# The scan's inverse products as 32x32 blocks, with GpSimd placing only the diagonal blocks of zt

## What is computed

```python
lower = jnp.where(strict, jnp.einsum('bnhid,bnhjd->bnhij', k_beta, k) * decay, 0.0)
t_inv = lax.linalg.triangular_solve(lower + eye, eye, left_side=True, lower=True, unit_diagonal=True)
...
def step(s, inp):
    q_i, val_i, kc_i, at_i, gl_i, kt_i = inp
    v_new = val_i - jnp.einsum('bhcd,bhde->bhce', kc_i, s)
    o = jnp.einsum('bhcd,bhde->bhce', q_i, s) + jnp.einsum('bhij,bhje->bhie', at_i, v_new)
    s = s * jnp.exp(gl_i)[..., None, None] + jnp.einsum('bhcd,bhce->bhde', kt_i, v_new)
    return s, o
xs = tuple(jnp.moveaxis(a, 1, 0) for a in (q_dec, value, k_cum, attn, g_last, k_tail))
_, o = lax.scan(step, s0, xs)
```

## Time and profile before

| | us |
|---|---|
| median of 3 runs (2006.83 to 2012.97) | 2008.74 |
| the profiled execution | 2008.84 |
| its span | 2007.1 |
| PE busy | 1934.2 (96%) |
| DVE busy | 1034.9 (52%) |
| ACT busy | 588.4 (29%) |
| POOL busy | 545.0 (27%) |

### The profile page before, as it was taken

The page is one execution under the profiler, slowest core; times in us unless marked ns, Lnnn a source line. Parts: engine busy times, 40 slices in busy tenths (PEclk is TensorE's granted clock), DMA queues, the critical chain, the costliest instruction groups (busy, mean ns, idle before and its releaser), DMA issues.

```text
span 2007.1 us, 29418 instructions
## 1 busy us (share of the span) xinstructions
PE 1934.2 (96%) x11744; PEld 1562.7 (78%) x11744; DVE 1034.9 (52%) x1363; ACT 588.4 (29%) x952; POOL 545.0 (27%) x336
## 2 busy tenths in 40 slices
PE   8999999999999999999889999999999999999994
PEld 6777787677788887888667687788888888888883
DVE  2747643864459601777676429324242424242437
ACT  3434533334221211656421311222111212122112
POOL 1221122211122313344143824321212222121203
PEclk9999999999999998999999999999999999999997
DMA  6345672336553582686553632121212121211102
GB/s 161 62 101 129 165 171 81 84 93 167 137 145 100 133 235 85 188 239 202 180 172 116 205 105 61 35 63 31 63 31 63 31 63 32 62 38 56 48 5 84
DMA packets 339847, 211.86 MB, mean 106 GB/s; under 512 B 166140, under 2 KB 310140, under 8 KB 337696
## 3 DMA queue, kind: packets, MB, share of 16 engines
q1 hardware_dynamic: 264176, 156.38, 28.1%
q10 hardware_dynamic: 75568, 54.04, 9.4%
HBM read 151.27 MB, written 59.06 MB: 105 GB/s over the span
## 4 chain that ended last, share of the span: by engine, by line
PE 45%; DVE 3%; POOL 1%; DMA 1%; ACT 0%; issue 0%; SPq 0%; DVEq 0%; ACTq 0%
PE b_ps L154 11%; PE b_ps L155 11%; PE b_ps L156 11%; PE f_ps L154 4%; PE f_ps L155 4%; PE f_ps L156 4%; DMA o_raw<-in_w_out 1%; DVE l_stats L2277 1%; POOL x1lo L1764 1%; DVE y L2289 0%; DVE y L2274 0%; PE f_ps L1845 0%; POOL wo_lo L1770 0%; PE f_ps L1807 0%; POOL x1lo L1756 0%; PE f_ps L1882 0%
## 5 line engine op out<-in xcount | busy, mean ns | idle before, releaser
L154 PE MATMUL bank<-xhi,w_hi 128*128 128x512 f32 x976 | 393.2, 403 | 2.3 <-POOL w_lo L433 1.5
L155 PE MATMUL bank<-xlo,w_hi 128*128 128x512 f32 x976 | 385.8, 395 | 0.0
L156 PE MATMUL bank<-xhi,w_lo 128*128 128x512 f32 x976 | 385.7, 395 | 0.0
L433 POOL TENSOR_TENSOR w_lo<-w_raw,w_hi 128x1024 fp32r<-128x1024 f32 x61 | 167.9, 2753 | 600.3 <-ACT w_hi L799 600.3
L2249 DVE TENSOR_TENSOR bw_raw<-bw_raw,b_ps 128x512 f32<-128x512 f32 x42 | 28.9, 688 | 388.4 <-PE b_ps L156 380.1
L154 PEld LDWEIGHTS bank<-xhi,w_hi 128*128 128x128 f32 x976 | 183.7, 188 | 48.4 <-POOL w_lo L433 3.4
L156 PEld LDWEIGHTS bank<-xhi,w_lo 128*128 128x128 f32 x976 | 183.4, 188 | 44.5
L155 PEld LDWEIGHTS bank<-xlo,w_hi 128*128 128x128 f32 x976 | 183.6, 188 | 43.8 <-issue 1.7
L2257 DVE TENSOR_TENSOR y<-y,f_ps 128x512 f32<-128x512 f32 x320 | 200.5, 684 | 0.5
L1792 POOL TENSOR_TENSOR bw_split<-ff_raw_down,ff_hi_down 128x1024 fp32r<-128x1024 f32 x22 | 53.3, 2422 | 526.7 <-ACT ff_hi_down L2050 526.7
L154 PE MATMUL f_ps<-ff_hi_down,ff_hhi 128*128 128x512 f32 x352 | 142.3, 404 | 3.6 <-DVE ff_hlo L2268 3.6
(11 more groups left out here) (324 smaller groups left out, 3443.7 us busy)
## 6 DMA issues: line engine op xcount, KB each, us to landing
w_raw<-in_w_in ACTq DMA_DIRECT2D x61, 512.0 KB, 4.4
op<-opnd SPq DMA_DIRECT2D x16, 1152.0 KB, 5.5
u<-work ACTq DMA_DIRECT2D x68, 256.0 KB, 4.0
b_gate<-u SPq DMA_DIRECT2D x24, 512.0 KB, 3.6
ff_raw_gate<-in_ffn_gate SPq DMA_DIRECT2D x22, 512.0 KB, 4.0
ff_raw_up<-in_ffn_up SPq DMA_DIRECT2D x22, 512.0 KB, 5.4
ff_raw_down<-in_ffn_down SPq DMA_DIRECT2D x22, 512.0 KB, 5.9
opnd<-work SPq DMA_DIRECT2D x20, 512.0 KB, 5.7
```

The lines of the kernel that those rows point to most:

```text
L154: pe.matmul(out, w_hi, x_hi, start=first, stop=False)
L155: pe.matmul(out, w_hi, x_lo, start=False, stop=False)
L156: return pe.matmul(out, w_lo, x_hi, start=False, stop=last)
L433: pool.tensor_tensor(w_lo[b][:, :, :], w_raw[b][:, :, :], as_f32(w_hi[b][:, :, :]), ALU.subtract).then_inc(w_lo_done, 1)
```

## The change

The products are made with the 32x32 blocks themselves. The first one takes `corner` and `packed` as they were loaded, on partitions 0 to 31 and 64 to 95 (`upper`), and writes partitions 32 to 63 and 96 to 127 (`lower`); the second goes the other way. `join`, `inv` and `place_inverse` are gone. `ps_y` and `ps_z` have columns of their own in the bank. ACT copies the two 32-partition pieces of `ps_y`, DVE copies the two pieces of `ps_z` into the corner of `zt` instead of adding, and POOL copies the diagonal blocks into `zt`, whose zeros are set once at the start of the scan, where chunk 0 is now placed too. The second product waits for the `zt` copies of the chunk before; the transpose did so until now. Writers of `zt` wait for `ps_w` of two chunks back. Core of the diff:

```diff
-def place_inverse(pool, c, tiles, join_done, inv_done):
-    op, ar, sv, wv, packed, corner, inv, join = tiles
-    b, d = c % 2, c % DEEP
-    for k in (0, 64):
-        pool.tensor_copy(join[b][k:k + 32, :, NB:2 * NB], corner[d][k:k + 32, :, :]).then_inc(join_done, 1)
-    pool.wait_ge(join_done, c * 2 + 2)
-    for q in range(4):
-        rows, t0 = slice(32 * q, 32 * q + 32), NB * (q % 2)
-        pool.tensor_copy(inv[b][rows, :, :, t0:t0 + NB], packed[d][rows, :, :, :]).then_inc(inv_done, 1)
...
-            for b in range(2):
-                pool.memset(inv[b][:, :, :, :], 0.0).then_inc(early_cleared, 1)
-                pool.memset(join[b][:, :, :], 0.0).then_inc(early_cleared, 1)
...
-            place_inverse(pool, 0, early, early_join, early_placed)
...
-        ps_y = ps_z = ps_yz[:, 0:NPAIR * C].rearrange("p (u s) -> p u s", u=NPAIR)
+        ps_y, ps_z = (ps_yz[:, n * NPAIR * NB:(n + 1) * NPAIR * NB].rearrange("p (u s) -> p u s", u=NPAIR) for n in range(2))
+        upper = [slice(64 * e, 64 * e + NB) for e in range(2)]
+        lower = [slice(64 * e + NB, 64 * e + 2 * NB) for e in range(2)]
...
-                if c:
-                    pe.wait_ge(zt_done, c)
...
-                pe.wait_ge(join_done, c * 2 + 2)
-                pe.wait_ge(inv_done, c * 4 + 4)
+                pe.wait_ge(inv_landed[d], c // DEEP * 48 + 48)
                 for u in range(NPAIR):
                     for e in range(2):
-                        h = rwkv_rows(e)
-                        last = pe.matmul(ps_y[h, u, :], join[b][h, u, :], inv[b][h, 0, u, :], start=True, stop=True)
+                        last = pe.matmul(ps_y[lower[e], u, :], corner[d][upper[e], u, :], packed[d][upper[e], 0, u, :], start=True, stop=True)
...
-                pe.wait_ge(y_done, c + 1)
+                pe.wait_ge(y_done, c * 2 + 2)
                 pe.wait_ge(vt_done, c + 1)
+                if c:
+                    pe.wait_ge(zt_done, c * 2)
                 for u in range(NPAIR):
                     for e in range(2):
-                        h = rwkv_rows(e)
-                        last = pe.matmul(ps_z[h, u, :], y[b][h, u, :], inv[b][h, 1, u, :], start=True, stop=True)
+                        last = pe.matmul(ps_z[upper[e], u, :], y[b][lower[e], u, :], packed[d][lower[e], 1, u, :], start=True, stop=True)
...
-                dve.wait_ge(inv_done, c * 4 + 4)
-                dve.tensor_tensor(zt[b][:, :, :], ps_z, inv[b][:, 1, :, :], ALU.add).then_inc(zt_done, 1)
+                if c == 0:
+                    dve.wait_ge(zt_cleared, 2)
+                if c >= 2:
+                    dve.wait_ge(mm_w, c - 1)
+                for e in range(2):
+                    dve.tensor_copy(zt[b][upper[e], :, NB:2 * NB], ps_z[upper[e], :, :]).then_inc(zt_done, 1)
...
-                act.activation(y[b][:, :, :], ps_y, ACT.Copy).then_inc(y_done, 1)
+                for e in range(2):
+                    act.activation(y[b][lower[e], :, :], ps_y[lower[e], :, :], ACT.Copy).then_inc(y_done, 1)
...
+            for b in range(2):
+                pool.memset(zt[b][:, :, :], 0.0).then_inc(zt_cleared, 1)
+            pool.wait_ge(zt_cleared, 2)
...
-                if c:
-                    place_inverse(pool, c, tiles, join_done, inv_done)
+                if c >= 2:
+                    pool.wait_ge(mm_w, c - 1)
+                for e in range(2):
+                    for k, half in enumerate((upper[e], lower[e])):
+                        pool.tensor_copy(zt[b][half, :, k * NB:(k + 1) * NB], packed[d][half, 1, :, :]).then_inc(inv_done, 1)
```

More of the change, by code:

```diff
@@ L260, in scan_tiles @@
     packed, corner = loads("inv_packed", [2, NPAIR, NB]), loads("inv_corner", [NPAIR, NB])
-    inv, join = ([sb(f"{name}{b}", [P] + shape) for b in range(2)] for name, shape in (("inv", [2, NPAIR, C]), ("join", [NPAIR, C])))
-    return op, ar, sv, wv, packed, corner, inv, join
+    return op, ar, sv, wv, packed, corner
 def load_chunk(sp, c, tiles, opnd, xinv, landed, inv_landed):
-    op, ar, sv, wv, packed, corner, inv, join = tiles
+    op, ar, sv, wv, packed, corner = tiles
     b, row = c % DEEP, opnd[c]
@@ L387, in project_and_prepare @@
         inv_landed, inv_cleared, inv_stored = sem("inv_landed"), sem("inv_cleared"), sem("inv_stored")
-        early_landed, early_inv, early_cleared, early_join, early_placed = (sem("early_" + n) for n in ("landed", "inv", "cleared", "join", "placed"))
+        early_landed, early_inv = (sem("early_" + n) for n in ("landed", "inv"))
         inv_step = [sem(f"inv_step{k}") for k in range(2)]
@@ L434, in _ @@
             local.sweep(pool)
-            *_, inv, join = early
-            pool.wait_ge(inv_stored, 16 * 4 * R)
-            for b in range(2):
-                pool.memset(inv[b][:, :, :, :], 0.0).then_inc(early_cleared, 1)
-                pool.memset(join[b][:, :, :], 0.0).then_inc(early_cleared, 1)
-            pool.wait_ge(early_cleared, 4)
-            pool.wait_ge(early_inv, 48)
-            place_inverse(pool, 0, early, early_join, early_placed)
-            pool.wait_ge(early_placed, 4)
         @block.sync
@@ L1148, in scan_and_attend @@
         local.enter_context(nc.sbuf_tensor("scan_tiles", [P, sum(math.prod(t.shape[1:]) for group in tiles for t in group)], F32))
-        op, ar, sv, wv, packed, corner, inv, join = tiles
+        op, ar, sv, wv, packed, corner = tiles
         causal, attn = two("causal", [8, C]), two("attn", [2, 2, C])
         tok_g = two("tok_g", [2, 2, GD])
-        y, zt = two("y", [NPAIR, C]), two("zt", [NPAIR, C])
+        y, zt = two("y", [NPAIR, NB]), two("zt", [NPAIR, C])
         r_rw, r_g, w_g = two("r_rw", [4, C]), two("r_g", [2, GD]), two("w_g", [2 * GD])
@@ L1170, in scan_and_attend @@
         mm_m, mm_a, mm_y, mm_z, mm_r, mm_w, mm_s, mm_o = (sem("mm_" + n) for n in "mayzrwso")
-        masked, attn_done, inv_done, join_done, tok_done, y_done, zt_done = (
-            sem(n) for n in ("m_masked", "attn_done", "inv_done", "join_done", "tok_done", "y_done", "zt_done"))
+        masked, attn_done, inv_done, tok_done, y_done, zt_done = (
+            sem(n) for n in ("m_masked", "attn_done", "inv_done", "tok_done", "y_done", "zt_done"))
+        zt_cleared = sem("zt_cleared")
         r_rw_done, r_g_done, w_done, s_sum_done, s_rw_done, dec_done, s_g_done, o_done = (
@@ L1221, in _ @@
                     sp.wait_ge(mm_o, c - DEEP + 1)
-                    sp.wait_ge(zt_done, c - DEEP + 1)
+                    sp.wait_ge(zt_done, 2 * (c - DEEP + 1))
+                    sp.wait_ge(inv_done, 4 * (c - DEEP + 1))
                     load_chunk(sp, c, tiles, opnd, xinv, landed[b], inv_landed[b])
@@ L1288, in state @@
                 yield
-                pe.wait_ge(zt_done, c + 1)
+                pe.wait_ge(zt_done, c * 2 + 2)
+                pe.wait_ge(inv_done, c * 4 + 4)
                 pe.wait_ge(r_rw_done, c + 1)
@@ L1521, in _ @@
         def _(pool):
-            pool.sem_inc(join_done, 2)
-            pool.sem_inc(inv_done, 4)
             pool.memset(keys[:, :, 0:C], 0.0).then_inc(padded, 1)
             pool.memset(values[:, 0:C], 0.0).then_inc(padded, 1)
+            for b in range(2):
+                pool.memset(zt[b][:, :, :], 0.0).then_inc(zt_cleared, 1)
+            pool.wait_ge(zt_cleared, 2)
             def product(c):
```

## The result

The changed kernel takes 2016.02 us (median of 6 runs, 2014.53 to 2018.8) against 2008.88 of the kernel before: ratio 1.0036, 95% interval 1.0025 to 1.0047, or 7.2 us more (5.0 to 9.4). The forecast was 2013.6, with a range of 2008 to 2017.5. The time lies in the range. I gave "within 0.3%" 0.67 and "slower" 0.31; the ratio lies on the slower side of that line by 0.0006, but its interval holds the line, so which of the two it is stays open. That it is slower than the kernel before is clear of noise. The profiled execution of the changed kernel has a span of 2014.6 us.

What follows compares the result with a forecast made beforehand. A closed ScalarE-VectorE-PE chain of 10.77 us per chunk was taken as the bound, PE full but 0.16 ahead. Chunks +5.4 and start -0.6 gave +4.8 on 2008.84: 2013.6 us, range 2008 to 2017.5.

Steps and rivals of the forecast that it cites:

- within 0.3%: Outcome between 2002.7 and 2014.8 us, too close to tell from no change; chance 0.67.
- slower: Outcome above 2014.8 us; chance 0.31.
- ScalarE's copies: Two y copies on other start partitions lose three overlaps; w_g to at_own 1.28 instead of 0.90, +0.38 per chunk.
- The first rival: ScalarE's overlap stays despite changed partitions; 0.01 per chunk, hidden under at_top, time 2008.4; 15%.
- The chain: Closed chain per chunk through ScalarE, VectorE and PE: 3.44 + 0.04 + 2.67 + 0.06 + 4.56 = 10.77 us.
- PE's products: 32x32 inverse products on PE save 0 to 0.35 us each, off the chain except at the start.
- The second rival: 32-row matmuls do not run side by side, PE becomes the bound, +1.24 per chunk, time 2027; 5%.
- PE's wait for sv: At the ps_r product PE would wait 0.5 us or more for sv, instead of 0.16.
- POOL, DVE's zt, the new waits: POOL waits about 1.8 longer before s_dec; zt copies 0.17 longer, hidden before r_g; new waits lose nothing.
- Start, first and second chunk: Scan start -0.6 from narrower products at half clock; first y copy's chunk +0.43, second's +0.05.
- The third rival: Clock falls in the scan as PE idles; one ten-us stretch at half clock, about +4, 2017.6; 6%.
- a fall between 805 and 960: Sign that the forecast is wrong: the granted clock falls between 805 and 960 us in the profile.

Runs made afterwards that it cites:

- two of my experiments: Changed kernel with y in one copy (2008.28 us), and that kernel with at_vt's copy also moved behind the exponentials (2009.5 us); period 10.79 in both.
- one copy of y: Changed kernel with ScalarE's two 32-partition y copies put back into one of 128 partitions x 192 columns: 2008.28 us, ratio 1.0001 to the kernel before.
- the kernel with the quarter moved: Changed kernel with the load of the third quarter of keys, values and queries issued two chunks later: 2015.82 us, ratio 1.0036.
- the one with attn moved: Changed kernel with VectorE's two attn multiplications moved behind at_top and at_own, y still copied in two: 2014.21 us, ratio 1.0034.
- the product issued twice: Changed kernel with the 24 matmuls of the first corner product issued twice in every chunk: 2021.79 us, ratio 1.0062.
- the kernel with one copy and attn moved: Changed kernel with y in one copy and VectorE's attn multiplications moved behind at_top and at_own: 2005.07 us, ratio 0.9986.
- the one before with attn moved: Kernel before the change with only VectorE's attn multiplications moved behind at_top and at_own: 2008.18 us, ratio 1.0001.

## Why the prediction was right, and where its sum was short

**ScalarE's copies: right in size and cause.** Forecast 1.28 us from w_g to at_own and +0.38 a chunk; measured 1.28, and +0.36 in the period. The remaining 0.02 are gained back behind at_own: the last accumulator read ends 1.73 after at_own's start instead of 1.75. That this stretch of ScalarE sets the period shows in all fourteen profiled executions: from wv to at_own it is 1.31 to 2.29 us in a steady chunk, and from at_own to the next wv 9.07 to 9.10, whatever the kernel (medians of chunks 2 to 14). The cause is shown from three sides: same start, 0.21 each; other start, 0.35 each (0.51 for the halves of 384 columns); and an order of wv alone moves w_g by 0.12. The Trainium skill gives such a rule for VectorE ("VectorE: DVE Perf Modes", section "Two Vector instructions with no wait between them"), and ScalarE's copies in these runs agree with it. Tried were changes between 0, 32 and 96 and between 0 and 64, with input and output changing together; which of the two holds the next copy was not run. The overlap of about 93 ns that the Trainium skill names in "ScalarE: Activation LUTs", section "What ACT_TABLE_LOAD costs", agrees with w_g to y with one start (0.38 long, 0.28 apart) and not with copies on changing starts. The first rival, 2008.4, falls with that.

**The chain: right in its length, incomplete in its ways.** The forecast followed ScalarE from wv and mentioned at_top only as a bound for the first rival. In the kernel before two ways reached at_own within about 0.05 us of each other: at_own starts 0.21 behind at_vt there, with at_top the last to end, and 0.16 behind it once attn is moved out of VectorE's way, which shortened the period by 0.06. For the change it made no difference, as ScalarE's was the one that grew; for the way back it did: two of my experiments expected 10.4 and 10.6 from ScalarE's gain alone and got 10.79.

**PE's products: right in the saving, not in where PE waits.** The first takes 0.57 instead of 0.92, the upper bound of the saving (0.35), and nothing of it reaches the period: with one copy of y the period is that of before. The second rival (no side by side) falls: 24 matmuls still start 0.57 - 0.18 = 0.39 us apart from first to last. PE's wait for sv, forecast at 0.5 or more, is 0.32. PE now waits in other places ahead of it as well: in the same chunk its weight loads stand 0.23 us for wv, which they did not before, and three times 0.15 to 0.17 for at_score instead of once.

**POOL, DVE's zt, the new waits: right.** POOL waits 7.24 - 5.45 = 1.79 longer (forecast 1.8); r_g keeps its 0.79.

**Start, first and second chunk: right, where the clock held.** Scan start to the first wv is 12.77 instead of 13.41 us, -0.64 (forecast -0.6); the first product there takes 0.85 instead of 1.55. The match needed luck: PE also waits there for the load of at_values, by chance about as long in both (0.70 and 0.66 us), but between nothing and 2.49 us in other executions, and the way to the first wv lies between 12.16 and 13.56 in four executions with the changed kernel's start. Chunk 1 takes +0.04 (+0.05). Chunk 0 takes 12.58 in the kernel with the quarter moved, which leaves this chunk alone: +0.43, as forecast. In the profiled execution of the changed kernel it took 13.94.

**What the sum put at nothing: the clock and late instructions.** Forecast +4.8; measured +7.2 (5.0 to 9.4). In the trace the scan up to the last wv is 183.99 - 176.66 = 7.3 us longer. 4.3 of it are the forecast's terms with their measured sizes: 13 steady periods at 0.36, 0.43 and 0.04 in the first two, -0.64 at the start, less 0.2 that the kernel before itself lost in its chunk of 10.97. The other 3.0 are the two chunks with the half clock: 1.36 in chunk 0 and 1.66 in chunk 5. In chunk 5 a late instruction is part of it: one of 0.79 at the same place, without half clock, made the chunk 0.5 longer in two other executions (11.66 and 11.65), so I estimate 0.8 for this one of 1.07 and the rest for the clock. Outside this stretch the two executions differ by -2.0 ahead of the scan and by +2.2 behind it, where the changed kernel's has 6.83 us more at half clock. The third rival was this mechanism, with one ten-us stretch and +4 at 6%; what came were two of 3.41 us. The text had also named a fall between 805 and 960 as a sign against the forecast, and it showed.

The two profiled executions are no exceptions in this. The granted clock over the whole execution is on record for every run: 0.984 to 0.986 in the eleven of the changed kernel (mean 0.985), and 0.983 to 0.989 in 86 of the kernel before (mean 0.987). One stretch of 3.41 us at half clock lowers it by 0.0008, so I estimate two to three such stretches more in the changed kernel's runs; in the profiled pair it is four, two of them in the scan. Where they lie in the runs without a profile isn't on record, so how much of the median's excess over 4.3 the two in the scan make is not settled.

What brings the clock down is not settled either. Five executions have the wait of 1.33 us in chunk 0: the half clock follows in three (the changed kernel twice, and the one with attn moved: 13.94, 13.94, 14.10 us) and not in two (the product issued twice, and the quarter moved: 12.58 each). It also came once behind a shorter one, 0.92, in the kernel with one copy and attn moved (13.52), and did not behind the same 0.92 in the one with one copy alone (11.97). Late instructions stand in executions of kernels with the old products, too: in the one before with attn moved, the second product of chunk 11 made that chunk 11.71 us. Why they come late was not shown.

## What to carry to other kernels

Where ScalarE copies back to back on the critical way, count the changes of start partition before the elements: a copy of all 128 partitions with unused rows took 0.21 us in the row where two of 32 partitions took 0.69, and putting the halves in the order that ends on the next one's start was worth 0.1 us a chunk. Before trimming one way into a join, read when the other one arrives: here two lay about 0.05 us apart, and only trimming both paid. A sum built from steady periods needs a line of its own for the chunks that are not steady.

## What the runs showed that I had not expected

On ScalarE the overlap depends on the start partition, with sizes that are alike for copies of 192, 256 and 384 columns: about 0.10 us of overlap with one start, a gap of about 0.025 with another.

PE's instructions come late, without a semaphore, at the same few places of the program but not in each execution: 0.7 to 1.6 us in the first product of chunk 5 in six of the fourteen profiled executions, for one. Issuing 24 more small matmuls in a chunk, hidden by their time, went with five such chunks in one execution; the median of that kernel is 6.6 us higher.

A wait of PE of 1.33 us at one place was followed by 3.41 us at half clock in three executions and by full clock in two. What sets them apart was not found.
